# An even block with its prompt convolution in PSUM, its statistics on GpSimd and its gates moved, and a final norm taken row by row

## What is computed

```python
def even_mixer(h, hist_pool, hist_conv, start_pos, w_in, pool_w, pool_scale, conv_w, conv_b, ln_g, ln_b, w_out):
    z = jnp.einsum('btd,de->bte', h, w_in)
    a_in, a_gate, b_val, b_glu, b_gate = jnp.split(z, [W_A, 2 * W_A, 2 * W_A + W_B, 2 * W_A + 2 * W_B], axis=-1)
    a_full = jnp.concatenate([hist_pool.astype(a_in.dtype), a_in], axis=1)
    a = multiscale_pool_minus_self(a_full, start_pos)            # windows 2, 4, 8, 16 of 256 channels each
    a = jnp.einsum('btgc,gce->btge', a, pool_w).reshape(Bn, T, W_A) * pool_scale
    a = a * jax.nn.silu(a_gate)
    v = b_val * jax.nn.sigmoid(b_glu)
    v_full = jnp.concatenate([hist_conv.astype(v.dtype), v], axis=1)
    c = causal_dwconv(v_full, conv_w) + conv_b                   # 31 taps for each channel
    c = jax.nn.silu(layernorm(c, ln_g, ln_b)) * jax.nn.silu(b_gate)
    y = jnp.einsum('bte,ed->btd', jnp.concatenate([a, c], axis=-1), w_out)
    return y, a_full[:, -POOL_HIST:], v_full[:, -CONV_B_HIST:]

def rmsnorm(x, g):
    y = xf * lax.rsqrt(jnp.mean(xf * xf, axis=-1, keepdims=True) + EPS)
```

## Time and profile before

| what | us |
|---|---|
| runs, median of 3 | 2841.66 (2833.34 to 2842.91) |
| the profiled execution's own time | 2844.08 |
| its span, first to last instruction | 2842.3 |
| PE busy | 2505.6 (88%) |
| DVE busy | 1417.4 (50%) |
| POOL busy | 1288.6 (45%) |
| ACT busy | 430.9 (15%) |
| mean granted PE clock | 0.94 of full |
| even block: first to last matmul of its tiles | 57.8 to 956.6 |

### The profile page before, as it was taken

One profiled execution on the slowest core, in us unless ns is written; L12 is line 12 of the kernel. 1 busy time (PEld: TensorE's weight loads), 2 busy tenths in 40 slices (PEclk: granted clock), 3 DMA queues, 4 the chain that ended last, 5 costly groups with the idle time before them and its releaser, 6 DMA issues. The chain is left out here.

```text
span 2842.3 us, 37890 instructions
## 1 busy us (share of the span) xinstructions
PE 2505.6 (88%) x14918; PEld 2402.2 (85%) x14918; DVE 1417.4 (50%) x1582; ACT 430.9 (15%) x728; POOL 1288.6 (45%) x842
## 2 busy tenths in 40 slices
PE   4967879777699679999799999999999997799996
PEld 4967879777699669878799999999999996698886
DVE  5999999999744452332522232222313234523324
ACT  3110110101111320121310000000000003211212
POOL 2644444434355454345544444444444445543452
PEclk7988999889899799999899999999999997999998
DMA  2111111111121132233011111111111111322331
GB/s 90 53 37 44 48 47 49 45 30 45 53 73 57 41 109 78 68 114 111 24 48 45 42 44 45 45 41 45 45 45 41 45 44 38 112 78 67 114 111 63
DMA packets 224013, 168.55 MB, mean 59 GB/s; under 512 B 10746, under 2 KB 219138, under 8 KB 223922
## 3 DMA queue, kind: packets, MB, share of 16 engines
q1 hardware_dynamic: 214002, 156.78, 18.0%
q10 hardware_dynamic: 9920, 10.48, 1.1%
HBM read 152.29 MB, written 14.93 MB: 59 GB/s over the span
## 5 line engine op out<-in xcount | busy, mean ns | idle before, releaser
L146 POOL TENSOR_TENSOR w_hi<-w_raw,ones 128x512 fp32r<-128x512 f32 x404 | 574.3, 1421 | 1412.8 <-PE PS L210 1221.1
L210 PE MATMUL PS<-h_hi,w_hi 128*128 128x364 f32 x2880 | 645.7, 333 | 64.1 <-DVE e_V L827 39.1
L149 POOL TENSOR_TENSOR w_lo<-w_raw,w_hi 128x512 fp32r<-128x512 f32 x404 | 644.7, 1596 | 31.6
L210 PE MATMUL PS<-h_hi,w_lo 128*128 128x364 f32 x2880 | 641.9, 331 | 0.0
L210 PE MATMUL PS<-h_lo,w_hi 128*128 128x364 f32 x2880 | 640.9, 331 | 0.0
L210 PEld LDWEIGHTS PS<-h_hi,w_hi 128*128 128x128 f32 x2880 | 502.5, 190 | 68.9 <-DVE e_V L827 40.3
L210 PEld LDWEIGHTS PS<-h_hi,w_lo 128*128 128x128 f32 x2880 | 505.9, 190 | 0.0
L210 PEld LDWEIGHTS PS<-h_lo,w_hi 128*128 128x128 f32 x2880 | 505.1, 190 | 0.0
L850 DVE SCALAR_TENSOR_TENSOR e_C<-e_V,prm,e_C 128x1024 f32<-128x1024 f32 x240 | 321.8, 1341 | 0.3
L210 PE MATMUL PS<-y_hi,w_hi 128*128 128x364 f32 x1152 | 261.7, 336 | 62.2 <-ACT e_GS L701 26.0
L210 PEld LDWEIGHTS PS<-y_hi,w_hi 128*128 128x128 f32 x1152 | 201.6, 193 | 69.9 <-issue 44.9
(11 more groups left out here) (192 smaller groups left out, 2144.8 us busy)
## 6 DMA issues: line engine op xcount, KB each, us to landing
w_raw<-in_w_in_odd SPq DMA_DIRECT2D x128, 256.0 KB, 2.8
w_raw<-in_w_in_even SPq DMA_DIRECT2D x80, 256.0 KB, 2.9
a_KV<-in_cache_mem_k SPq DMA_DIRECT2D x64, 256.0 KB, 4.8
a_KV<-in_cache_mem_v SPq DMA_DIRECT2D x64, 256.0 KB, 4.6
w_raw<-in_w_out_even SPq DMA_DIRECT2D x32, 256.0 KB, 3.0
w_raw<-in_w_k SPq DMA_DIRECT2D x32, 256.0 KB, 2.8
w_raw<-in_w_v SPq DMA_DIRECT2D x32, 256.0 KB, 2.8
w_raw<-in_w_q SPq DMA_DIRECT2D x32, 256.0 KB, 2.8
```

Of the source, the lines that this page charges most:

```text
L146: c.nc.gpsimd.tensor_tensor(by_128(c.Wh[:, s, :]), by_128(c.Wraw[:, s % RAW, :]), ones, ALU.mult).then_inc(self.w_hi, 1)
L149: c.nc.gpsimd.tensor_tensor(c.Wl[:, s, :], c.Wraw[:, s % RAW, :], c.Wh[:, s, :].bitcast(F32), ALU.subtract).then_inc(self.w_split, 1)
L210: mm = pe.matmul(ps[:, q, 0:PART], w, a[:, q * PART:(q + 1) * PART], start=first and n == 0, stop=last and n == 2)
```

## The change

- **Plan of the tiles.** From the second pair on, outa g-1 stands behind the first tile (glu) of the next even chunk. Odd chunks go glu, ain, val, agate. After the last pair: bgate 0, outa 3, bgate 1, the sums, bgate 2 and 3; then bgate 4+g ahead of each outb g.
- **Prompt convolution.** The accumulator of the prompt taps is PSUM banks 6 and 7; only the prompt's 1024 columns are tapped one by one. ACT copies the result to SBUF.
- **Sample convolution.** One product over 16 taps and one over 15 (`sample_conv`), each with a sum over the taps behind it, and one instruction that joins them.
- **Statistics.** ACT makes the first chunk's, POOL adds chunks 1 to 6 between its weight splits, DVE adds the last.
- **States.** All 16 histories are loaded and turned ahead of the block's norm. The new states are turned and copied behind bgate 2 and later, and stored from SP's queue. The copies of new sample columns go from DVE to ACT.
- **Gates.** the bgate tiles go to five buffers instead of two; `yb_high` and `gate` alternate on ACT.
- **Final norm.** The squares and their sums at the end of the second cross block are gone. Each 128 rows are transposed, ACT squares them with a sum, takes the root, DVE inverts it and multiplies, all from PSUM.

```diff
@@ even_plan
-        order += [(n, 2 * g) for n in ("glu", "val", "ain", "agate")]
+        j = 2 * g
         if g:
-            order += [("outa", g - 1, k) for k in range(KD)]
-        order += [(n, 2 * g + 1) for n in ("glu", "val", "ain", "agate")]
-        order += [("pool", 2 * g), ("pool", 2 * g + 1)]
-    order += [("bgate", 0), ("bgate", 1)]
-    order += [("sum", 0), ("sum", 1)]
-    order += [("outa", 3, k) for k in range(KD)]
+            order += [("glu", j)] + [("outa", g - 1, k) for k in range(KD)] + [(n, j) for n in ("val", "ain", "agate")]
+        else:
+            order += [(n, j) for n in ("glu", "val", "ain", "agate")]
+        order += [(n, j + 1) for n in ("glu", "ain", "val", "agate")]
+        order += [("pool", j), ("pool", j + 1)]
+    order += [("bgate", 0)] + [("outa", 3, k) for k in range(KD)]
+    order += [("bgate", 1), ("sum", 0), ("sum", 1), ("bgate", 2), ("bgate", 3)]
     for g in range(4):
-        if g < 3:
-            order += [("bgate", 2 * g + 2), ("bgate", 2 * g + 3)]
-        order += [("outb", g, k) for k in range(KD)]
+        order += [("bgate", 4 + g)] + [("outb", g, k) for k in range(KD)]
@@ block_even, gpsimd
-            G.split_all(pool, 116)
+            def add_stats(j):
+                pool.wait_ge(squared, j)
+                pool.wait_ge(stats, 2 * j)
+                nc.gpsimd.tensor_tensor(S1[:, :], S1[:, :], CB[:, j % 2, :], ALU.add).then_inc(stats, 1)
+                nc.gpsimd.tensor_tensor(S2[:, :], S2[:, :], SQ[:, :], ALU.add).then_inc(stats, 1)
...
+                if kind == "glu" and j % 2 == 0 and j >= 4:
+                    add_stats(j - 2)
+                elif kind == "agate" and j % 2 == 0 and j:
+                    add_stats(j - 1)
+                elif tile == ("bgate", 0):
+                    add_stats(KD - 2)
@@ block_even, scalar
+            for j in range(KD):
+                history(j)
+            norm.scalar_root(act)
...
+            def convolved(j):
+                act.wait_ge(cv, CONV * (j + 1))
...
+                s.activation(CB[:, j % 2, 0:T].rearrange("p (a n) -> p a n", a=2), c.PS[:, 6:8, :],
+                             ACT.Copy).then_inc(acc_read, 1)
@@ block_even, vector
+                acc = c.PS[:, 6:8, :]
+                for n in range(first, last):
+                    window = V[:, n:n + T].rearrange("p (a n) -> p a n", a=2)
...
+                        v.scalar_tensor_tensor(acc, window, tap, acc, ALU.mult, ALU.add).then_inc(cv, 1)
+            def sample_conv(j):
...
+                for i, (first, taps) in enumerate(((0, FRONT), (FRONT, CONV - FRONT))):
...
+                    start = by_batch(VS[:, j, first:first + TS, :])
+                    windows = bass.AP(start.tensor, start.offset, [list(d) for d in start.ap] + [[NB, taps]])
...
+                    v.tensor_tensor(products, windows, weights, ALU.mult).then_inc(s_cv, 1)
+                    v.tensor_reduce(SA[i], products, AX_X, ALU.add).then_inc(s_cv, 1)
...
             for g in range(4):
+                j = 2 * g
+                value(j)
+                conv(j, 0, 8)
+                sample_conv(j)
+                pooling(j)
+                conv(j, 8, 10)
+                pooled_low(j)
+                conv(j, 10, CONV)
+                j += 1
+                pooling(j)
+                value(j)
+                conv(j, 0, 2)
+                pooled_low(j)
+                conv(j, 2, 11)
+                ya(j - 1)
+                conv(j, 11, 13)
+                y_low(j - 1, j - 1)
+                ya(j)
+                conv(j, 13, 15)
+                y_low(j, j)
+                sample_conv(j)
+                at = 15
+                for k in range(KD):
+                    add("outa", g, k)
+                    conv(j, at, at + 1)
+                    at += 1
+                conv(j, at, CONV)
@@ block_final
+            for t in range(tiles):
+                act.wait_ge(turned, t + 1)
+                nc.scalar.activation(SQ[0:rows(t), t % 2, :].rearrange("p (h n) -> p h n", h=2), banks(t), ACT.Square,
+                                     scale=1.0 / 32, accum_out=MS[0:rows(t), t:t + 1]).then_inc(summed, 1)
+                act.wait_ge(summed, t + 1)
+                nc.scalar.activation(RS[0:rows(t), t:t + 1], MS[0:rows(t), t:t + 1], ACT.Sqrt,
+                                     bias=c.eps[0:rows(t), 0:1]).then_inc(rooted, 1)
...
+                nc.vector.reciprocal(RS[0:n, t:t + 1], RS[0:n, t:t + 1]).then_inc(inverted, 1)
+                nc.vector.scalar_tensor_tensor(YN[0:n, t, :].rearrange("p (h n) -> p h n", h=2), banks(t), RS[0:n, t:t + 1],
+                                               GB[0:n, :].rearrange("p (h n) -> p h n", h=2), ALU.mult,
+                                               ALU.mult).then_inc(scaled, 1)
@@ block_cross, gpsimd and scalar
-            norm.next_sums(pool)
+            if layer == 0:
+                norm.next_sums(pool)
```

More of the change, by code:

```diff
@@ L617, in _ @@
                         u += 1
-                if kind == "outa" and j == 3 and tile[2] == 0 or kind == "outb" and tile[2] == 0 and j < 3:
-                    for n in (0, 1) if kind == "outa" else (2 * j + 2, 2 * j + 3):
-                        if n < 2:
-                            sp.wait_ge(stored[n], 16 * KD // 2)
-                            sp.wait_ge(stats, 3 * (7 + n))
-                        else:
-                            sp.wait_ge(yb, n - 1)
-                        sp.dma_start(CB[:, n % 2, :], scratch[n]).then_inc(c_in[n % 2], 16)
@@ L626, in _ @@
-            sp.wait_ge(rows_stored, 80 * KD)
+                if tile == ("bgate", 3):
+                    for n in range(2):
+                        sp.wait_ge(stored[n], 16 * KD // 2)
+                        reload(n, stats, 2 * KD)
+                elif kind == "outb" and tile[2] == 0 and j < 3:
+                    for n in (2 * j + 2, 2 * j + 3):
+                        reload(n, yb, n - 1)
+                for n in stores_after.get(tile, ()):
+                    store_tail(n)
+            for n in range(2):
+                sp.wait_ge(rows_stored[n], 80 * KD // 2)
@@ new lines, in _ @@
+            for tile in order:
+                kind, j = tile[0], tile[1]
+                if kind in ("glu", "val", "ain", "agate", "bgate"):
+                    split(2)
+                elif kind == "pool" and j % 2 == 0:
+                    split(1)
+                elif kind in ("outa", "outb") and tile[2] == 0:
+                    split(4)
+                if kind == "glu" and j % 2 == 0 and j >= 4:
[4 more added lines that the diff above has]
+                    add_stats(KD - 2)
@@ L690, in _ @@
                         pe.wait_ge(G.w_split, u + 1)
-                    Ah, Al = (Mh, Ml) if kind == "pool" else (c.Yh, c.Yl)
-                    G.pair_tile(pe, u, k % 2, n % 2, before, Ah, Al)
+                    G.pair_tile(pe, u, k % 2, n % 2, before, c.Yh, c.Yl)
                     u += k % 2
+                for m in tail_after.get(tile, ()):
+                    tails(m)
         @block.scalar
@@ L965, in _ @@
             v.tensor_scalar(V[:, 0:TP], V[:, 0:TP], 0.0, None, ALU.max).then_inc(ln_var, 1)
-            for k in range(3):
-                add("outa", 3, k)
             dve.wait_ge(ln_std, 1)
```

501 lines of the change are left out of this document (265 added, 236 removed).

## The result

| what | before | after |
|---|---|---|
| runs, median | 2841.26 of 4 (2833.34 to 2842.91) | 2724.97 of 4 (2722.95 to 2725.78) |
| the profiled execution's own time | 2844.08 | 2722.95 |
| its span | 2842.3 | 2721.2 |
| DVE busy | 1417.4 | 1315.5 |
| PE busy | 2505.6 | 2479.5 (91%) |

The ratio to before is 0.9595 (95% interval 0.9576 to 0.9614): 4% faster. The forecast was 2690, and 2725 lies outside its range of 2664 to 2722.

A forecast was written before the change was run, and what follows sets the result against it. DVE's taps were taken to bound the first stretch, PE the second, with an idle end. Terms -113 (first stretch), -28 (second), +2 (start), -14 (final norm) sum to -153 on 2844.08: forecast 2690 us, range 2664 to 2722.

The forecast's parts named there:

- The taps: First stretch, DVE's prompt convolution: each tap accumulating in PSUM takes 1.31 us, 248 are 325 us, 150 us saved.
- the rival of the free wait: Waiting for the tap right ahead costs nothing, so taps take 1.19 us and the kernel 2666; chance 0.10.
- The sample convolution: New DVE work in the first stretch: 6 us for each chunk, plus 48; 18 more if the stride halved the rate.
- The ring: First stretch: DVE and PE bind each other at about 134 us per pair of chunks, 537 instead of 650, minus 113.
- Products of the sample above 2 us: Sign that the forecast is wrong: the sample convolution's products on DVE taking over 2 us, against 1.2 assumed.
- The walk of one pair: First stretch, one pair stepped through from its `value`: PE waits 2.5 and 5 us for low parts; pair about 134.
- The statistics: First stretch: statistics leave DVE for all but one chunk, minus 24 us of DVE's work.
- Second stretch: Last tap to the even block's end: 194 us instead of 222, minus 28, with three PE stalls of 3.7 us.
- Final norm: Kernel's end after the last add to X: ACT paces tiles at 1.6 us; 27 us instead of 41.1, minus 14.
- PSUM or the strided products are dearer: Rival: taps 0.1 us dearer cost 25 us, the halved stride rate 18; kernel 2715 to 2735; chance 0.22.
- DVE's accumulate at half rate: Rival at the taps (L964): reading and writing the same PSUM banks takes turns; kernel 2957, slower than before; chance 0.03.
- POOL late for PE: Rival: POOL's adds delay weight splits that PE needs, stalling it 5 us six times; kernel 2720; chance 0.07.

The follow-up runs named there:

- acc_sbuf: The kernel after, with the prompt convolution's accumulator in the finished chunk's SBUF buffer instead of two PSUM banks; 2820.64 us (0.9928).
- s_step1: The kernel after, with the sample convolution's products reading with a step of 1 instead of 8 (wrong positions); 2717.32 us (0.9561).
- lo_small: The kernel after, with POOL's second split instruction writing 4 columns instead of 512 from the even block's fifth unit on; 2706.75 us (0.953).
- stats_dve: The kernel after, with the first stretch's six pairs of statistics adds moved back from POOL to DVE; 2729.88 us (0.9609).
- ya_end: The kernel after, with a pair's first gated result made after fewer taps and the taps left out put at the pair's end; 2726.45 us (0.961).
- act_order: The kernel after, with ACT making both high parts of a pair before the next gate, for g = 1 and 2; 2712.23 us (0.9551).

## Why the prediction was wrong

**The taps: right.** 1.288 each, none held up beside POOL (none of 240 over 1.291), starts 1.325 apart in a run of them (seven in 9.24), forecast 1.31; the taps and the idle steps ahead of them are 327 us, forecast 325. acc_sbuf shows why. The medians are 1290 in PSUM and 1285 in SBUF. A tap starts 0.035 behind the end of the last, so the rival of the free wait is out: against the 1.19 of a tap followed by another kind the wait did cost here.

**The sample convolution: the term that failed most.** I took 6 us for a chunk, "two products and two sums of about 1000 columns at 1.2 each", and left the dear stride out of the sum ("if that halved the rate, it would be 18 more"). The groups sum to 68 us of busy time, 8.5 for a chunk, and 9.0 with the steps between: 24 us more. Of these some 14 are the step of 8 (16 times 0.9, s_step1), 8 the join held by POOL (8 times 1.03, lo_small). "Products of the sample above 2 us" was one of the forecast's own signs of being wrong, and it came.

**POOL: a cost that I only counted on the other side.** I wrote of POOL that it "will no longer be held by the taps", and took that as help; apart from "some meeting with POOL" in the 6 us above, what POOL does to DVE stood at nothing. But the instructions that remain in SBUF meet it. The pooling groups, low parts with them, rise from 71.6 to 92.4 us. Two changes could do it: POOL has 32.6 us of adds more, and its splits are shorter and denser since no tap holds them (1.45 mean, L149 before 2136). Of the first, stats_dve takes 10 us back (82.3), about half. The second is not borne out: in acc_sbuf the taps hold the splits again (L149 2038), and the pooling groups are no cheaper (98.3). lo_small, with the adds in place and half of the splitting gone, has 80.7, so splits and DVE do meet there; where the other half of the 21 us comes from is open, and the new order of DVE's steps is a rival that no run tests. One POOL add can cost nearly its whole length:

```profile
287.21 2.48 POOL L681 TENSOR_TENSOR e_S<-e_S,e_SQ 128x1092 f32<-128x1092 f32 x1
```

The low part that starts 0.15 behind it (the first of the lines below) takes 3.49 us instead of 1.29.

**The ring: an average over four pairs that differ.** The walk of one pair put the odd `value` at 67.5 from the even one (done with two taps at 71.4); it was 61.4, 67.1, 77.5 and 82.4. With the window grows the pooling ahead of it, and a short pair gives nothing to a long one: pair 0 is near PE's 127 (128.87 busy of 130.84), pairs 1 to 3 are DVE's. The walk had PE wait for the second gated result's low part in each pair; no wait for L1035 is in this stretch. It missed that PE's next glu needs the bank that `ya` reads, behind nine taps (16.1 us of waits, 4.5 in pair 1):

```profile
287.36 3.49 DVE L1019 TENSOR_TENSOR y_lo<-e_P,y_hi 128x1092 fp32r<-128x1092 f32 x1
290.88 11.89 DVE L964 SCALAR_TENSOR_TENSOR PS<-e_V,prm,PS 128x1024 f32<-128x1024 f32 x9
302.68 1.35 DVE L1029 SCALAR_TENSOR_TENSOR e_P<-PS,prm,e_GS 128x1092 f32<-128x1092 f32 x1
304.09 1.28 PE L210 MATMUL PS<-h_hi,w_hi 128*128 128x364 f32 x3 [4.55 <-DVE e_P L1029]
```

But by ya_end that wait costs nothing while DVE's sum sets the pair. In numbers the whole miss of 34 us in this stretch is DVE's work: 123 us less than 632.95 would have been 510 busy, and 547 was measured, while its idle time (24) is even a little under the 27 that the forecast of 537 left. As busy time, the sample convolution is 20 above its 48 and the pooling 21 above nothing. The statistics gave 20 and not 24: the forecast took in the last chunk's two adds, which lie behind the stretch. The taps gave 5 more than 150. (The forecast's "about 527" takes its 123 from the stretch's 650 and not from DVE's 632.95; its sum went by 134 a pair and did not use it.)

**Second stretch: right in its mechanism.** The three stalls came where forecast, 3.52, 3.53 and 5.13 against 3.7 each, and act_order took two of them away. The steps to the sums took 10.8, forecast 11. The 7 us that are missing lie behind them, 38.9 against 36 and 151.4 against 147; part of it is PE's turning of the new states there (32 small matmuls, 7.5 us busy but partly overlapped, and a wait of 1.1 for ACT), which my sum left out. The rest is open.

**Final norm: mis-sized by 4.** ACT takes 1.33 for a tile, not 1.6 (a square starts at 2705.92, the next at 2707.25), since the accumulator's 0.19 and the root's 0.29 overlap with their neighbours. That makes DVE the pace and not ACT: its products start 1.39 apart, and 8 of these steps are 11.1 us where the sum had nine of 1.6:

```profile
2705.92 1.01 ACT L486 ACTIVATE y_squares<-PS 128x1024 f32<-128x1024 f32 x1
...
2706.38 1.28 DVE L500 SCALAR_TENSOR_TENSOR y_rows<-PS,y_rstd,g_rows 128x1024 f32<-128x1024 f32 x1
2706.83 0.19 ACT L486 ACTIVATION_READ_ACCUMULATOR y_squares<-PS 128x1 f32 x1
2707.05 0.29 ACT L489 ACTIVATE y_rstd<-y_means,eps 128x1 f32<-128x1 f32 x1
2707.25 1.00 ACT L486 ACTIVATE y_squares<-PS 128x1024 f32<-128x1024 f32 x1
...
2707.77 1.28 DVE L500 SCALAR_TENSOR_TENSOR y_rows<-PS,y_rstd,g_rows 128x1024 f32<-128x1024 f32 x1
```

**The rivals.** The time fell where "PSUM or the strided products are dearer" had put it (2715 to 2735), and that is mostly luck: of its reasons the stride was dear and PSUM was not, and the stride explains 7 to 10 of the 35 us. DVE's accumulate at half rate did not occur (its arithmetic was 2 off: 248 times 1.07 is 265). POOL late for PE did not occur, no wait for w_lo stands among PE's waits in the even block. What POOL's instructions cost DVE had no rival of its own.

## What to carry to other kernels

When an instruction is no longer held up by another engine, ask which ones are left that it can hold up, down to those of 64 columns and of one: each can cost the whole of the other's instruction (the join took 1.31 us beside an L149 of 1.29, against 0.28 in lo_small; a one-column step, L1008, took up to 2.32 with a median of 0.154). Two engines that hold each other up can also fall into step, so that such a meeting comes at the same place every time (the join and L149, 8 of 8). Price a strided read at the dear end until a row shows otherwise (2.05 us at least with a step of 8, 1.16 with a step of 1). Where a loop's work grows from turn to turn, sum the maximum of each turn's bounds, not the maximum of the means, and expect that only the turns and parts in which an engine is the bound give back what is taken from it.

## What the runs showed of the hardware

- A DVE instruction of 64 columns with two SBUF inputs took 0.28 us behind a POOL instruction of 0.20 (L990 behind L150, lo_small) and 1.31 behind one of 1.29 (L988 behind L149, after), each begun 0.07 before it.
- DVE reading SBUF with a step of 8 fp32 elements took 2.05 us at least (L981, after), with a step of 1 1.16 (s_step1; least of the two forms in each case).
- The sum over taps (L983), with one SBUF input, stayed between 1152 and 1221 ns in the kernel after, though in each of the 16 a POOL split ran beside it for over 1 us.
- A tap that accumulates in PSUM, reading and writing the same two banks, had a median 5 ns above that of one in SBUF (1290 in after, 1285 in acc_sbuf).
- The first tap of a chunk, with one input in SBUF and no accumulator to read, was dearer into PSUM: 1348 ns (L960 in after, 1346 to 1351) against 812 into SBUF when nothing holds it (acc_sbuf, least 811).
- A POOL split (L146) that ran beside a DVE product with two SBUF inputs (the second L981 of a chunk, in after) ended 1.07 to 1.11 us behind the product's end, 8 times of 8, wherever it had been released.
